# Pairing the later modulation loads and sums, with a re-ordered first stage, in a two-block transformer kernel

## The chip, the cores and the metric

One Trainium2 chip, one core. The metric is the device time of one execution in microseconds, the median of the runs shown. The engines named below: PE multiplies matrices (PEld is its weight load), DVE and ACT work element by element, POOL sets constants, SP issues nearly all DMAs from a queue of its own.

## The reference, cut to what matters

Two transformer blocks of two layers each, on 256 latent and 256 context tokens of width 1024, all in float32. What the change touches is the adaptive norm of the first block: a condition vector gives a shift, a scale and a gate of 1024 values each, for each of two layers, for latent tokens and for context tokens.

```python
def adaln_terms(cond, w_ada, b_ada):
    m = jax.nn.silu(cond) @ w_ada + b_ada        # [1024] @ [1024, 3072]
    return jnp.split(m, 3, axis=-1)
...
for li in range(DEPTH):
    shift_l, scale_l, gate_l = adaln_terms(c, ada_w[li], ada_b[li])
    shift_c, scale_c, gate_c = adaln_terms(c_ctx, ada_w[li], ada_b[li])
    xl = rms_norm(h_lat, norm_w[li]) * (1.0 + scale_l[:, None, :]) + shift_l[:, None, :]
    xc = rms_norm(h_ctx, norm_w[li]) * (1.0 + scale_c) + shift_c
    out_l, out_c = mixer(xl, xc, ...)            # projections, attention, output projection
    h_lat = h_lat + gate_l[:, None, :] * out_l
```

## The kernel before, in words

Every engine runs one program that is written out by hand; semaphores join them. The work is a sequence of weight chunks r = 0, 1, 2, ... of 128x1024 floats (512 KB). For each chunk SP loads it into one of four `raw` buffers (`load_raw`, L757), ACT rounds it into a high part (`split_hi`, L839), DVE subtracts to get the low part (`split_lo`, L1341), and PE forms three products of high and low parts (L2088 to L2090). SP may load chunk r only when the low part of chunk r - 4 is done: `lo_done` must have reached r - 3. The queue of SP is strictly in order, so whatever stands behind a waiting load waits too.

The modulation weights `ada_w` (25 MB) are read as 24 quanta of 256 columns; each is loaded as two halves of 512 KB (`load_ada`, L768) into four buffers `ada_raw`. PE sums a quantum with the condition as a 32-column stationary operand: four products side by side, one in each quarter of the PSUM rows, for each half (`condition`, L2183). A float32 product shows as two records in the trace. ACT copies the sum out (`ada_evacuate`, L881), PE transposes it (`condition_turn`, L2199), DVE adds the four parts and the bias (`ada_finish`, L1482).

The first stage. The first eight quanta give scale and shift of layer 0. x arrives in four tiles of 128 tokens and is transposed column tile by column tile (`turn_x`, L2260: eight groups of four transposes into two PSUM banks `tr`, each copied out by ACT). The norm factors come from DVE, which squares the four tiles as they land. Then four "pairs" follow. Pair p needs quanta 2p and 2p + 1; DVE makes `amod`, then for each of four half tiles (two column tiles, latent and context) a product `ntmp` (L1405), ACT makes the high part `h_hi` (L854), DVE the low part `h_lo` (L1415), and PE multiplies all this with chunk p of the "av" weights (`value_part`: 24 products of 512 columns a pair). In `modulated_norm` the low part of chunk p is made in one piece of 1024 columns; for pairs 1 to 3 it is made between `ada_finish(2p)` and `ada_finish(2p + 1)`.

PE's order in the kernel before, in a pair p with 0 < p < 3: `condition(2p+2)`, six products, `condition_turn(2p+2)`, `condition(2p+3)`, six products, `condition_turn(2p+3)`, twelve products.

After the first stage the sixteen later quanta are summed in eight pairs, at chunk slots 6, 8, ..., 20 (`condition_pair`): PE sums quantum 8 + 2j into columns 0 to 255 of a PSUM bank and quantum 9 + 2j into columns 256 to 511, projects the chunk, and then transposes the bank. SP's order is: four times (two quanta, one chunk), chunks 4 to 7, right behind chunk 7 eleven small and middling loads (constants, vectors for lambda, layer norm, `a_ws`; L788 to L800), chunk 8, modulation pair 0, chunks 9 and 10, modulation pair 1, and so on.

Of the kernel before, what the change touches and what calls it, by code (L numbers as in the profile page):

```python
# [170 lines left out]
NADA = 3 * KT  # L171
ADA_COLS = 256
ADA_FIRST, ADA_ALL, NADA_RAW = 8, 24, 4

# [239 lines left out]
def build_program(nc, t, out):  # L414

    with ExitStack() as ctx:
        def sb(name, shape, dt=F32):
            return ctx.enter_context(nc.sbuf_tensor(name, shape, dt))
# [4 lines left out]
        def sem(name):  # L423
            return ctx.enter_context(nc.semaphore(name))


        with nc.sbuf_tensor("ada_raw", [P, NADA_RAW, KT, ADA_COLS], F32) as ada_raw:
            pass
        m_hi, m_lo = sb("m_hi", [P, KT * TOK], F32R), sb("m_lo", [P, KT * TOK], F32R)
        cond32 = sb("cond32", [P, KT, 32])  # L430
# [107 lines left out]
            sem("misc_in"), sem("stored"))  # L538
        rows_in = sem("rows_in")
        ones_set, eps_set, lam_set = sem("ones_set"), sem("eps_set"), sem("lam_set")  # L540
# [100 lines left out]
        def source_at(r):  # L641

            if r >= RB:
# [11 lines left out]
                       (V_KVN, t["c_kv_norm_w"]))  # L655

        def ada_bank(n):

            return (sc[:, 1, :], ac[:, :])[n % 2]
# [84 lines left out]
        def _(sp):  # L744
# [14 lines left out]
            def load_ada(n):  # L759
# [6 lines left out]
                for half in range(2):  # L766
                    tiles = slice(4 * half, 4 * half + 4)
                    sp.dma_start(ada_raw[:, n % NADA_RAW, tiles, :], src[:, tiles, :])\  # L768
                        .then_inc(ada_in[half][n % NADA_RAW], 16)

            for r in range(HELD):
                load_ada(2 * r)
                load_ada(2 * r + 1)
                load_raw(r)
            for r in range(HELD, RB + LAYERS_2 * C2):
# [8 lines left out]
                if r - 2 in ADA_OF_SLOT:  # L784
                    for n in ada_pair(ADA_OF_SLOT[r - 2]):
                        load_ada(n)
                if r == 7:
# [34 lines left out]
        def _(act):  # L822
# [77 lines left out]

            turned(0, vec[:], tr[:, 0, 0:V_END])
            act.wait_ge(tr_free, 1)
# [3 lines left out]
            def x_turned_to(k):  # L906
                use = TR1_OF[("x", k)]
                turned(use, x_t[:, k, :], tr[:, use % 2, :])

# [4 lines left out]

            for k in range(3):
                x_turned_to(k)
            ada_evacuate(0)
            x_turned_to(3)
            ada_evacuate(1)
            x_turned_to(4)  # L920
            split_hi(0)
            modulated_hi(0, 0)
            x_turned_to(5)
            x_turned_to(6)
            modulated_hi(0, 1)
            x_turned_to(7)
            for pair in range(1, 4):
                ada_evacuate(2 * pair)
                ada_evacuate(2 * pair + 1)
                split_hi(pair)  # L930
                modulated_hi(pair, 0)
                modulated_hi(pair, 1)
            nc.scalar.activation(small[:, 60:61], ones[:, 0:1], ACT.Gelu)
# [392 lines left out]
        def _(dve):  # L1326
# [8 lines left out]
            def split_lo(r):  # L1335
# [6 lines left out]
                last.then_inc(lo_done, 1)  # L1342

            rotations = [0]

# [147 lines left out]
            def modulated_norm(layer, v0, v1, chunk=None):  # L1493
                dve.wait_ge(rs_set, layer + 1)
                for v in range(v0, v1 + 1):
                    u = 2 * KT * layer + v
                    if v < v1:
                        k, half = norm_tile(layer, v)
                        norm_tmp(u, k, (LAT, CTX)[half], amod[:, layer, half, k:k + 1], (LAT, CTX)[half])
                    if chunk is not None and v == v0 + 1:  # L1500
                        split_lo(chunk)
                    if v > v0:
                        k, half = norm_tile(layer, v - 1)
                        norm_lo(u - 1, k, (LAT, CTX)[half], mod[:, layer, k, half:half + 1])

            norm_rsqrt(0, 4)
            for pair in range(4):
                ada_finish(2 * pair)
                if pair:
                    split_lo(pair)  # L1510
                ada_finish(2 * pair + 1)
                dve.wait_ge(ada_set, 2 * pair + 2)
                modulation(0, 2 * pair, 2 * pair + 2, 2 * pair + 2)
                modulated_norm(0, 4 * pair, 4 * pair + 4, chunk=None if pair else 0)
            split_lo(HELD)
# [563 lines left out]
        def _(pe):  # L2079
# [107 lines left out]
            def condition_pair(j):  # L2187

                g = G1_OF[("ada", j)]
                group_bank_free(pe, g, None)  # L2190
                for e, n in enumerate(ada_pair(j)):
                    last = condition_sums(n, bank(g)[:, ADA_COLS * e:ADA_COLS * e + ADA_COLS])
                last.then_inc(proj_done, 1)
# [38 lines left out]
            pe.wait_ge(ident_in, 16)  # L2232
            pe.wait_ge(vec_in, 16 * 9)
            nc.tensor.transpose(tr[:, 0, 0:V_END], vec_rows[0:V_END, :], const[0:V_END, K_ID:K_ID + V_END]).then_inc(tr_done, 1)
            pe.wait_ge(ones_set, 1)
            for n in range(4):
                pe.wait_ge(x_in[n], 16)
            def value_part(name, j, e, tiles=range(4)):
                c = L0_CHUNKS.index((name, j))
                k, (wh, wl) = 2 * j + e, split_views(c)  # L2240
                if e == 0:
                    pe.wait_ge(lo_done, c + 1)
                for n in tiles:
                    tok = slice(P * n, P * n + P)
                    if name == "av":
                        pe.wait_ge(n_lo, 2 * k + n // 2 + 1)
                    if k == 0 and n == 3:
# [14 lines left out]

            turn_x(0)
            turn_x(1)
            turn_x(2)
            pe.wait_ge(cond_set, 1)
            condition(0)
            turn_x(3)
            spread(0, 4)
            condition_turn(0)  # L2270
            condition(1)
            turn_x(4)
            condition_turn(1)
            turn_x(5)
            turn_x(6)
            condition(2)
            turn_x(7)
            for pair in range(4):
                if 0 < pair < 3:
                    condition(2 * pair + 2)  # L2280
                value_part("av", pair, 0, (0, 1))
                if pair < 3:
                    condition_turn(2 * pair + 2)
                    condition(2 * pair + 3)
                value_part("av", pair, 0, (2, 3))
                if pair < 3:
                    condition_turn(2 * pair + 3)
                value_part("av", pair, 1)

# [454 lines left out]
```

## Time and profile before

| what | value |
|---|---|
| median of 3 runs | 1055.52 us (1054.69 to 1056.17) |
| profiled execution | 1054.3 us |
| its span, first to last instruction | 1052.2 us |
| PE busy | 1032.1 us, 98% of the span |
| DVE, ACT busy | 733.7 us, 591.1 us |
| DMA | 165.38 MB, mean 157 GB/s |

The page is made from one execution. The span leaves out what lies around the first and the last instruction, 2.1 us here. PE's busy time counts the modelled ends of pipelined products, so short waits can hide in it; the start of one record to the start of the next is the sharper measure, and the timeline gives it.

### The profile page before, as it was taken

What the parts mean: (1) busy time and instruction counts of PE and PEld (TensorE: products, weight loads), DVE (VectorE), ACT (ScalarE), POOL (GpSimd) and SP (SyncE); (2) the same over time, 40 slices, a digit from 0 to 9 for tenths busy, and PEclk for the clock granted to TensorE, in tenths of its full rate; (3) what the DMA queues carried; (4) which work ended last, traced back from release to release, by engine and by line L of the source; (5) the groups of instructions that cost most, each with busy time, mean ns of one, the idle gap of its engine ahead of it and who ended that gap; (6) DMA issues with size and microseconds to landing.
All of it is one profiled execution on the core that took longest, in us unless ns stands there. A gap on an engine that the chain in (4) does not pass through costs nothing.

```text
span 1052.2 us, 17814 instructions
## 1 busy us (share of the span) xinstructions
PE 1032.1 (98%) x6745; PEld 879.4 (84%) x6745; DVE 733.7 (70%) x1569; ACT 591.1 (56%) x1188; POOL 2.6 (0%) x10
## 2 busy tenths in 40 slices
PE   6999999999999999999999999999999999999997
PEld 3677777788986779989898988889989898888886
DVE  4635576786687657797689775658797688665565
ACT  4534245553365556567667664446578767655444
POOL 0000000000000000000000000000000000000000
PEclk9999999999999999999999999999999999999999
DMA  9998661223333225565555556666455456555662
GB/s 328 274 345 264 183 197 41 81 61 100 100 101 91 61 61 151 137 179 141 141 141 160 160 161 193 188 188 182 132 160 161 128 147 166 155 168 179 184 218 81
DMA packets 203693, 165.38 MB, mean 157 GB/s; under 512 B 7117, under 2 KB 172729, under 8 KB 203609
## 3 DMA queue, kind: packets, MB, share of 16 engines
q1 hardware_dynamic: 203088, 163.28, 53.0%
q8 instruction: 54, 0.88, 0.4%
q0 software_dynamic: 192, 0.66, 0.2%
q10 hardware_dynamic: 328, 0.32, 0.1%
q14 instruction: 31, 0.25, 0.1%
HBM read 163.18 MB, written 1.05 MB: 156 GB/s over the span
## 4 chain that ended last, share of the span: by engine, by line
PE 90%; DVE 6%; ACT 2%; issue 1%; DMA 0%; ACTq 0%; DVEq 0%
PE pj L2088 24%; PE pj L2090 23%; PE pj L2089 23%; DVE w_lo L1341 2%; PE tr L2657 1%; PE pj L2183 1%; PE ac L2450 1%; PE tr L2316 1%; PE ac L2593 1%; PE sc L2436 1%; PE sc L2304 1%; PE ac L2330 1%; ACT w_hi L839 1%; PE sc L2439 1%; PE ac L2596 0%
## 5 line engine op out<-in xcount | busy, mean ns | idle before, releaser
L1341 DVE TENSOR_TENSOR w_lo<-raw,w_hi 128x1024 fp32r<-128x1024 f32 (+2 forms) x258 | 309.4, 1202 | 154.5 <-ACT w_hi L839 153.4
L839 ACT ACTIVATE w_hi<-raw 128x1024 fp32r<-128x1024 f32 (+2 forms) x258 | 267.6, 1040 | 97.4 <-PE pj L2090 90.2
L2088 PE MATMUL pj<-h_hi,w_hi 128*128 128x256 f32 (+1 forms) x960 | 297.1, 309 | 0.5 <-DVE m_lo L1747 0.2
L2090 PE MATMUL pj<-h_hi,w_lo 128*128 128x256 f32 (+1 forms) x960 | 290.5, 303 | 0.0
L2089 PE MATMUL pj<-h_lo,w_hi 128*128 128x256 f32 (+1 forms) x960 | 290.3, 302 | 0.0
L2088 PEld LDWEIGHTS pj<-h_hi,w_hi 128*128 128x128 f32 x960 | 183.2, 191 | 16.5 <-issue 8.4
L2090 PEld LDWEIGHTS pj<-h_hi,w_lo 128*128 128x128 f32 x960 | 183.2, 191 | 7.2
L2089 PEld LDWEIGHTS pj<-h_lo,w_hi 128*128 128x128 f32 x960 | 183.4, 191 | 6.3
L2088 PE MATMUL pj<-w_hi,h_hi 128*128 128x512 f32 x344 | 137.3, 399 | 0.4 <-DVE h_lo L1415 0.4
L2090 PE MATMUL pj<-w_hi,h_lo 128*128 128x512 f32 x344 | 134.2, 390 | 0.0
L2089 PE MATMUL pj<-w_lo,h_hi 128*128 128x512 f32 x344 | 134.2, 390 | 0.0
L2088 PEld LDWEIGHTS pj<-w_hi,h_hi 128*128 128x128 f32 x344 | 64.6, 188 | 17.4 <-issue 4.9
L2090 PEld LDWEIGHTS pj<-w_hi,h_lo 128*128 128x128 f32 x344 | 64.6, 188 | 13.9
L2089 PEld LDWEIGHTS pj<-w_lo,h_hi 128*128 128x128 f32 x344 | 64.7, 188 | 12.2
L2088 PE MATMUL pj<-m_hi,w_hi 128*128 128x256 f32 (+1 forms) x160 | 51.5, 322 | 1.1 <-DVE work L1761 0.8
L2090 PE MATMUL pj<-m_hi,w_lo 128*128 128x256 f32 (+1 forms) x160 | 50.4, 315 | 0.0
L2089 PE MATMUL pj<-m_lo,w_hi 128*128 128x256 f32 (+1 forms) x160 | 50.3, 315 | 0.0
L860 ACT ACTIVATE prob_t<-tr 128x512 f32<-128x512 f32 (+2 forms) x56 | 26.2, 518 | 42.6 <-PE tr L2316 40.3
L2088 PE MATMUL pj<-w_hi,m_hi 128*128 128x512 f32 x104 | 40.7, 392 | 0.0
L2090 PE MATMUL pj<-w_hi,m_lo 128*128 128x512 f32 x104 | 40.5, 390 | 0.0
L2089 PE MATMUL pj<-w_lo,m_hi 128*128 128x512 f32 x104 | 40.5, 389 | 0.0
L2088 PEld LDWEIGHTS pj<-m_hi,w_hi 128*128 128x128 f32 x160 | 30.4, 190 | 5.0 <-DVE work L1761 1.7
(376 smaller groups left out, 1479.6 us busy)
## 6 DMA issues: line engine op xcount, KB each, us to landing
raw<-in_w_in_dram SPq DMA_DIRECT2D x152, 512.0 KB, 3.8
ada_raw<-in_ada_w_dram SPq DMA_DIRECT2D x48, 512.0 KB, 8.4
raw<-in_even_w_in_dram SPq DMA_DIRECT2D x28, 512.0 KB, 7.0
raw<-in_w_branch_dram SPq DMA_DIRECT2D x24, 512.0 KB, 3.6
raw<-in_w_out_dram SPq DMA_DIRECT2D x16, 512.0 KB, 4.3
raw<-in_odd_w_in_dram SPq DMA_DIRECT2D x11, 512.0 KB, 4.0
raw<-in_even_w_out_dram SPq DMA_DIRECT2D x8, 512.0 KB, 3.8
raw<-in_odd_w_out_dram SPq DMA_DIRECT2D x8, 512.0 KB, 3.9
```

The lines of the kernel that those rows point to most:

```text
L839: last = nc.scalar.activation(hi, src, ACT.Copy)
L860: nc.scalar.activation(dst, src, ACT.Copy).then_inc(tr_free, 1)
L1341: last = nc.vector.tensor_tensor(lo, src, hi.bitcast(F32), ALU.subtract)
L2088: nc.tensor.matmul(dst, lh, rh, start=first, stop=False)
L2089: nc.tensor.matmul(dst, lh, rl, start=False, stop=False)
L2090: return nc.tensor.matmul(dst, ll, rh, start=False, stop=final)
L2183: last = nc.tensor.matmul(sums[32 * c:32 * c + 32, :], cond32[:, 4 * half + c, :], ada_raw[:, n % NADA_RAW, 4 * half + c, :], start=half = ...
L2304: nc.tensor.matmul(sc[:, a, unit_cols(u)], q_e[rows, h, P * i:P * i + P], k_e[rows, h, keys], start=True, stop=True).then_inc(sc_done, 1)
L2316: last = nc.tensor.transpose(tr[:, use % 2, P * j:P * j + P], src[:, P * j:P * j + P], ident)
L2330: last = nc.tensor.matmul(ac[:, P * i:P * i + P], prob_t[:, u % 2, P * j:P * j + P], v_e[:, n, P * h:P * h + P], start=(j == 0), stop=(j = ...
L2436: nc.tensor.matmul(sc[:, e, :], qn_o[:, 2 * hp + e, q], kn_o[:, 2 * hp + e, :], start=True, stop=False)
L2439: last = nc.tensor.matmul(sc[:, e, :], qr_o[rows, hp, q], kr_o[rows, :], start=False, stop=True)
```

## The change

It has three parts.

1. The first stage starts in another order. PE transposes the first five column tiles of x token tile by token tile, as each lands, into five banks (`x_bank`: the two `tr` banks and the three `pj` banks), and the small vectors go to bank `ac`; the other three column tiles follow after the first condition sums. PE's, ACT's and DVE's orders in the four pairs change: in pair p PE does six products, turn(2p+2), six products, condition(2p+3), six products, turn(2p+3), six products, condition(2p+4).
2. The low part of chunks 0 to 3 is made in two halves of 512 columns (`split_lo_half`), after the second and after the fourth `ntmp` of its pair. PE's products wait on the first half for the first column tile (`lo_half`) and on the second half (`lo_done`) for the other.
3. The sixteen later quanta are loaded in pairs: two transfers of 1 MB (rows of 512 columns) in place of four of 512 KB, into `ada_wide`, which takes the place of `ada_raw`; PE sums 512 columns with one product in place of two of 256 columns.

```diff
+X_EARLY = 5
...
+        def x_bank(k):
+            return pj[:, k - 2, :] if 2 <= k < X_EARLY else tr[:, TR1_OF[("x", k)] % 2, :]
...
+            def load_ada_pair(j):
+                n = ada_pair(j)[1]
+                sp.wait_ge(*sums_ready(n - NADA_RAW))
+                q = ADA_QUANTUM[n - 1]
+                c0 = ADA_COLS * (q % 12)
+                src = t["ada_w"][q // 12].rearrange("(k p) m -> p k m", p=P)[:, :, c0:c0 + 2 * ADA_COLS]
+                for half in range(2):
+                    tiles = slice(4 * half, 4 * half + 4)
+                    sp.dma_start(ada_wide[:, j % 2, tiles, :], src[:, tiles, :]).then_inc(ada_in[half][2 * (j % 2)], 16)
...
                 if r - 2 in ADA_OF_SLOT:
-                    for n in ada_pair(ADA_OF_SLOT[r - 2]):
-                        load_ada(n)
+                    load_ada_pair(ADA_OF_SLOT[r - 2])
... (ACT, after the first four column tiles of x)
             ada_evacuate(0)
-            x_turned_to(3)
+            x_turned_to(4)
+            x_turned_to(5)
             ada_evacuate(1)
-            x_turned_to(4)
             split_hi(0)
+            x_turned_to(6)
             modulated_hi(0, 0)
-            x_turned_to(5)
-            x_turned_to(6)
+            ada_evacuate(2)
             modulated_hi(0, 1)
             x_turned_to(7)
             for pair in range(1, 4):
-                ada_evacuate(2 * pair)
                 ada_evacuate(2 * pair + 1)
                 split_hi(pair)
                 modulated_hi(pair, 0)
+                if pair < 3:
+                    ada_evacuate(2 * pair + 2)
                 modulated_hi(pair, 1)
... (DVE)
+            def split_lo_half(r, e):
+                dve.wait_ge(hi_done, r + 1)
+                part = slice(e * WEL // 2, (e + 1) * WEL // 2)
+                (src, hi, lo), = split_pieces(r)
+                nc.vector.tensor_tensor(lo[:, part], src[:, part], hi[:, part].bitcast(F32), ALU.subtract)\
+                    .then_inc((lo_half, lo_done)[e], 1)
...
-                    if chunk is not None and v == v0 + 1:
-                        split_lo(chunk)
+                    if chunk is not None and v in (v0 + 1, v0 + 3):
+                        split_lo_half(chunk, (v - v0) // 2)
...
                 ada_finish(2 * pair)
-                if pair:
-                    split_lo(pair)
                 ada_finish(2 * pair + 1)
...
-                modulated_norm(0, 4 * pair, 4 * pair + 4, chunk=None if pair else 0)
+                modulated_norm(0, 4 * pair, 4 * pair + 4, chunk=pair)
... (PE)
-                for e, n in enumerate(ada_pair(j)):
-                    last = condition_sums(n, bank(g)[:, ADA_COLS * e:ADA_COLS * e + ADA_COLS])
+                for half in range(2):
+                    pe.wait_ge(ada_in[half][2 * (j % 2)], 16 * (ADA_FIRST // NADA_RAW + j // 2 + 1))
+                    for c in range(4):
+                        last = nc.tensor.matmul(bank(g)[32 * c:32 * c + 32, :], cond32[:, 4 * half + c, :],
+                                                ada_wide[:, j % 2, 4 * half + c, :], start=half == 0, stop=half == 1)
...
+            for i in (0, 2, 1, 3):
+                if i == 3:
+                    pe.wait_ge(vec_in, 16 * 9)
+                    nc.tensor.transpose(ac[:, 0:V_END], vec_rows[0:V_END, :], const[0:V_END, K_ID:K_ID + V_END])\
+                        .then_inc(tr_done, 1)
+                pe.wait_ge(x_in[i], 16)
+                for k in range(X_EARLY):
+                    last = nc.tensor.transpose(x_bank(k)[:, P * i:P * i + P], x_tok[:, i, P * k:P * k + P], ident)
+                    if i == 3:
+                        last.then_inc(tr_done, 1)
...
             for pair in range(4):
-                if 0 < pair < 3:
-                    condition(2 * pair + 2)
                 value_part("av", pair, 0, (0, 1))
                 if pair < 3:
                     condition_turn(2 * pair + 2)
-                    condition(2 * pair + 3)
                 value_part("av", pair, 0, (2, 3))
                 if pair < 3:
+                    condition(2 * pair + 3)
+                value_part("av", pair, 1, (0, 1))
+                if pair < 3:
                     condition_turn(2 * pair + 3)
-                value_part("av", pair, 1)
+                value_part("av", pair, 1, (2, 3))
+                if pair < 2:
+                    condition(2 * pair + 4)
```

## Rows read from the trace of the kernel before

**Rows 1.** The page: busy us, share of the span, instructions.
```profile
PE 1032.1 (98%) x6745; PEld 879.4 (84%) x6745; DVE 733.7 (70%) x1569; ACT 591.1 (56%) x1188; POOL 2.6 (0%) x10
```

**Rows 2.** Waits of PE over the whole span: us in total, times, longest.
```profile
PE tr L2234 <- DMA scr<-in_c_kv_norm_w_dram: 8.9, 1, 8.9
...
PE sc L2183 <- DMA ada_raw<-in_ada_w_dram: 0.5, 1, 0.5
...
PE pj L2088 <- DVE h_lo L1415: 0.4, 1, 0.4
```

**Rows 3.** Timeline of PE in the first stage: start us, us.
```profile
28.53 0.39 PE L2089 MATMUL tr<-w_lo,h_hi 128*128 128x512 f32 x1
28.76 0.39 PE L2090 MATMUL tr<-w_hi,h_lo 128*128 128x512 f32 x1
29.07 1.07 PE L2183 MATMUL sc<-ada_raw,cond 128*32 128x256 f32 x16
...
37.45 1.07 PE L2183 MATMUL sc<-ada_raw,cond 128*32 128x256 f32 x16
...
46.34 0.47 PE L2088 MATMUL pj<-w_hi,h_hi 128*128 128x512 f32 x1 [0.44 <-DVE h_lo L1415]
```

**Rows 4.** SP's issues: start us, us the issue took.
```profile
17.37 1.32 SPq L768 DMA_DIRECT2D ada_raw<-in_ada_w_dram  x1
...
44.03 0.37 SPq L757 DMA_DIRECT2D raw<-in_even_w_in_dram  x1
...
50.28 0.61 SPq L800 DMA_DIRECT2D prob<-in_a_ws_dram  x1
51.67 0.38 SPq L757 DMA_DIRECT2D raw<-in_even_w_in_dram  x1
...
55.12 0.86 SPq L768 DMA_DIRECT2D ada_raw<-in_ada_w_dram  x1
```

**Rows 5.** DMA landing of the issues at 17.37, then 55.12: us after the issue.
```profile
ada_raw<-in_ada_w_dram SPq DMA_DIRECT2D x1, 512.0 KB, 10.9
...
ada_raw<-in_ada_w_dram SPq DMA_DIRECT2D x1, 512.0 KB, 8.8
```

**Rows 6.** Timeline of DVE around the last pair of the first stage.
```profile
42.78 1.23 DVE L1341 TENSOR_TENSOR w_lo<-raw,w_hi 128x1024 fp32r<-128x1024 f32 x1 [2.02 <-ACT w_hi L839]
43.92 0.17 DVE L1482 TENSOR_REDUCE mod<-ac 128x4 f32<-128x16 f32 x1
...
44.59 0.87 DVE L1405 SCALAR_TENSOR_TENSOR ntmp<-x_t,amod,sc 128x256 f32<-128x256 f32 x2
45.71 0.49 DVE L1415 SCALAR_TENSOR_TENSOR h_lo<-ntmp,mod,h_hi 128x256 fp32r<-128x256 f32 x1 [0.25 <-ACT h_hi L854]
```

**Rows 7.** DVE groups by form: busy us, mean ns of one.
```profile
L1582 DVE TENSOR_TENSOR m_lo<-work,m_hi 128x512 fp32r<-128x512 f32 x8 | 5.2, 685 | 0.7 <-ACT m_hi L999 0.7
```

**Rows 8.** Windows: length, granted clock, DMA share, GB/s.
```profile
50.00:51.00 1.00, 1.00 0.35 131
53.00:54.00 1.00, 1.00 0.89 255
58.00:62.00 4.00, 1.00 1.10 348
63.00:65.00 2.00, 1.00 1.06 385
```

**Rows 9.** Timeline of PE at the first later modulation pair.
```profile
62.91 1.93 PE L2183 MATMUL pj<-ada_raw,cond 128*32 128x256 f32 x32
64.77 0.50 PE L2088 MATMUL pj<-h_hi,w_hi 128*128 128x512 f32 x1
```

**Rows 10.** PEld at the first modulation sum, sets of four side by side.
```profile
12.60 0.20 PEld L2183 LDWEIGHTS sc<-ada_raw,cond 128*32 128x32 f32 x4 [0.23 <-issue]
13.03 0.20 PEld L2183 LDWEIGHTS sc<-ada_raw,cond 128*32 128x32 f32 x4 [0.23 <-issue]
```

**Rows 11.** The line of the x transposes: ns min/median/max, first and last start.
```profile
L2260 PE MATMUL tr<-const,work x32: 272/300/474, 9.3 to 20.6; 128*128 128x128 f32 x32
```

More of the change, by code:

```diff
@@ L428, in build_program @@
             pass
+        with nc.sbuf_tensor("ada_wide", [P, NADA_RAW // 2, KT, 2 * ADA_COLS], F32) as ada_wide:
+            pass
         m_hi, m_lo = sb("m_hi", [P, KT * TOK], F32R), sb("m_lo", [P, KT * TOK], F32R)
@@ L538, in build_program @@
             sem("misc_in"), sem("stored"))
-        rows_in = sem("rows_in")
+        rows_in, lo_half = sem("rows_in"), sem("lo_half")
         ones_set, eps_set, lam_set = sem("ones_set"), sem("eps_set"), sem("lam_set")
@@ L899, in _ @@
                 nc.scalar.dma_start(vec_rows[c0:c0 + src.shape[0], :], src).then_inc(vec_in, 16)
-            turned(0, vec[:], tr[:, 0, 0:V_END])
+            turned(0, vec[:], ac[:, 0:V_END])
             act.wait_ge(tr_free, 1)
@@ L907, in x_turned_to @@
                 use = TR1_OF[("x", k)]
-                turned(use, x_t[:, k, :], tr[:, use % 2, :])
+                turned(use, x_t[:, k, :], x_bank(k))
             def value_evacuate(name, n):
@@ L913, in value_evacuate @@
                 nc.scalar.activation(dst, value_bank(name, n), ACT.Gelu if name == "av" else ACT.Copy).then_inc(value_free, 1)
-            for k in range(3):
+            for k in range(4):
                 x_turned_to(k)
             ada_evacuate(0)
-            x_turned_to(3)
+            x_turned_to(4)
+            x_turned_to(5)
             ada_evacuate(1)
-            x_turned_to(4)
             split_hi(0)
+            x_turned_to(6)
             modulated_hi(0, 0)
-            x_turned_to(5)
-            x_turned_to(6)
+            ada_evacuate(2)
             modulated_hi(0, 1)
@@ L2232, in _ @@
             pe.wait_ge(ident_in, 16)
-            pe.wait_ge(vec_in, 16 * 9)
-            nc.tensor.transpose(tr[:, 0, 0:V_END], vec_rows[0:V_END, :], const[0:V_END, K_ID:K_ID + V_END]).then_inc(tr_done, 1)
+            for i in (0, 2, 1, 3):
[8 more added lines that the diff above has]
+                        last.then_inc(tr_done, 1)
             pe.wait_ge(ones_set, 1)
-            for n in range(4):
-                pe.wait_ge(x_in[n], 16)
             def value_part(name, j, e, tiles=range(4)):
@@ L2240, in value_part @@
                 k, (wh, wl) = 2 * j + e, split_views(c)
-                if e == 0:
+                if e == 0 and name == "av":
+                    pe.wait_ge(lo_half, j + 1)
+                else:
                     pe.wait_ge(lo_done, c + 1)
@@ L2246, in value_part @@
                         pe.wait_ge(n_lo, 2 * k + n // 2 + 1)
+                    if name == "av" and k == 0 and n == 0:
+                        pe.wait_ge(tr_free, TR1_OF[("x", X_EARLY - 1)] + 1)
                     if k == 0 and n == 3:
@@ L2261, in turn_x @@
                 last.then_inc(tr_done, 1)
-            turn_x(0)
-            turn_x(1)
-            turn_x(2)
             pe.wait_ge(cond_set, 1)
             condition(0)
-            turn_x(3)
             spread(0, 4)
             condition_turn(0)
+            turn_x(5)
             condition(1)
-            turn_x(4)
+            turn_x(6)
             condition_turn(1)
-            turn_x(5)
-            turn_x(6)
+            turn_x(7)
             condition(2)
-            turn_x(7)
             for pair in range(4):
-                if 0 < pair < 3:
-                    condition(2 * pair + 2)
                 value_part("av", pair, 0, (0, 1))
```

## The prediction

> **What bounds the kernel now.** I read the page first: PE is busy for 1032.1 of 1052.2 us [rows 1]. So an edit pays only where PE waits, or where PE itself gets less to do. Next the waits of PE: 8.9 us until the first vectors land, then nothing above 0.8 us; among the rest 0.5 us on a modulation quantum and 0.4 us on `h_lo` [rows 2]. All the time that scheduling can win lies before 52 us.
>
> Then the timeline of PE in the first stage. One product of 512 columns takes 0.23 us from start to start; the condition sum of pair 1 starts at 29.07 and that of pair 2 at 37.45, so a pair takes 8.38 us [rows 3]. A pair's work is 24 products (5.5), two sums of 1.1 each and two turns of 0.25, with 0.1 for each of two switches: 8.4 us. PE is the bound inside the stage. Only the last pair waits: its first product starts at 46.34 after 0.44 us [rows 3].
>
> Last, SP. Chunk 7 is issued at 44.03, the eleven loads behind it end at 50.28 + 0.61 = 50.89, chunk 8 goes at 51.67, and the last transfer of modulation pair 0 at 55.12 [rows 4]. Why 44.03: the low part of chunk 3 is done at 42.78 + 1.23 = 44.01 [rows 6], and SP waits for just that. The last transfer of pair 0 lands 8.8 us after its issue [rows 5], at 63.92. PE starts that pair at 62.91, needs the last quarter about 1.4 us later at 64.3, and is through at 64.77 [rows 9]. **PE runs into the first later pair with 0.4 us to spare.** The reader is to see this: a low part that PE does not wait for sets when SP may go on.
>
> **Part 1, the first stage.** The transposes before the first sum get cheaper, but condition(4) needs its second half, which is issued at 17.37 and lands 10.9 us later [rows 4, 5], at 28.27. Before, PE comes to it at 29.07 [rows 3]. After, I lay the steps out with the durations above: PE gets there at about 27.5, sums the first half, waits 0.3 us and is through at 28.8, 1.3 us ahead of before. This lead is then spent. In the new order a pair's second turn stands six products before its end, not twelve. From turn(2p+1) the path is: turn and hand-over 0.44, DVE from the reduction to `ntmp` 44.59 - 43.92 = 0.67 [rows 6], two `ntmp` 0.79, half a low part 0.61 (a 128x512 subtraction is 0.685 from start to end [rows 7], 0.61 to the next one, as 1.23 stands to 1.14 in [rows 6]), `h_lo` 0.49 [rows 6], hand-over 0.06: 3.05 us. PE has six products left, and a sum in pairs 0 and 1: 1.45 + 1.1 after the turn's 0.24. So:
> - pair 1 starts at 28.8; six products, turn, six products, sum, six products = 1.45 x 3 + 0.24 + 1.1 = 5.7, so turn(5) is at 34.5;
> - pair 2 starts at 34.5 + 3.05 = 37.5 (PE waits 0.3), turn(7) is at 43.2;
> - pair 3 starts at 43.2 + 3.05 = 46.25 (PE waits 1.35).
>
> Before it started at 46.34 [rows 3]. The first stage ends where it did: **0.0 us**, with 0.5 either way for the hand-overs.
>
> **Part 2, the half low parts.** In the last pair DVE now does, from `ntmp` at 43.2 + 0.44 + 0.67 = 44.3: two `ntmp`, a half, `h_lo`, `ntmp`, `h_lo`, `ntmp`, then the second half. That is 0.79 + 0.61 + 4 x 0.395 = 2.98, so it starts at 47.3 and is done at 48.0. Before, the whole low part was done at 44.01 [rows 6]. `lo_done` reaches 4 **4.0 us later**, and chunk 7 is issued at 48.0 instead of 44.03. Behind it in SP's queue stand the eleven loads, chunk 8 and modulation pair 0. The eleven take 6.86 us of issuing, so chunk 8 goes at 54.9 (its own wait, the low part of chunk 4, was over at 51.67 before [rows 4] and moves little). PE does not wait for chunk 7 itself: its first use is two chunks further on, so for it the delay costs nothing.
>
> For pair 0 it costs this. The issue is 3.2 us later (4.0 less the 0.78 us that SP idled before chunk 8). The landing could move by that or by the full 4.0: the queues are nearly full in both cases, at 0.89 of an engine's share at 53 us [rows 8], so most of the gap closed in SP's queue does not shorten the line. I take 3.6. Rows of 512 columns move faster: 385 GB/s at 63 to 65 us, when chunks 9 and 10 with their 2 KB rows are on the way, against 348 at 58 to 62, when the 1 KB rows of pair 0 are [rows 8]. For the 2.1 MB of a pair that is 6.0 against 5.6, so -0.4 (bounds 0 and -0.45). The last half lands at 63.92 + 3.2 = 67.1. PE then has 0.95 us of sums left, because half of the pair's work hangs on the last transfer, no longer a quarter: it is through at 68.1, where the row has 64.77 [rows 9]. **+3.3 us** (bounds: 67.7, so +2.9, and 68.9, so +4.1). What follows at that slot is late alike: ACT copies the sum out later, and chunk 10's high part behind it; DMA and PE then run with the distances of before, and no wait of 0.5 us or more follows in which PE could give the time back [rows 2].
>
> The Trainium skill (DMA: Bandwidth & Descriptors, section "Bandwidth", under "Measured") asks for transfers of 1 MiB or more for 75% of peak, and gives 2.0 us plus bytes at 436 GB/s for one. Here 512 KB transfers already stream at 348 GB/s, since the queue holds several at once [rows 8]. By the page's formula four small ones, one after another, would cost 12.8 us and two large ones 8.8, and pair 0 would come 4 us earlier; by the rows it is 0.4.
>
> **Part 3, sums of 512 columns.** 32 records take 64.77 - 62.91 = 1.86 us [rows 9], four side by side 0.232. Is that columns or instructions? At the first sum PE still runs at half its clock: sets of four start 0.43 apart, 12.60 and 13.03 [rows 10], twice 0.215. So at least 0.215 of 0.232 is columns passing, which a wider product does not save. Merged, sets of four take 0.43 to 0.46, four of them 1.72 to 1.86: a gain of 0 to 0.14 a pair. I take 0.08, times eight: **-0.6 us** (0 to -1.1). Would instructions bind, a pair's 1.86 would halve and the kernel win 7 us; the doubling at half clock speaks against it.
>
> **The sum.** 0.0 + 3.3 - 0.6 = +2.7. On the profiled execution's own 1054.3 that is 1057.0. The median of the runs shown lies 1.2 above it, so 1055.5 + 2.7 = 1058.2.
>
> **The rivals.**
> - *The late loads are made good before pair 0* (the other side). Place: the stretch of the eleven small loads, where the DMA share is only 0.35 at 50 us [rows 8]. If pair 0 owes its landing to other work in the queues and not to SP's issue, the delay vanishes. It decides at a landing of 63.9 or earlier, half a sum before PE would otherwise be through. Then only part 3 is left: 1055.5 - 0.6 = 1054.9. For it: slack in the queues between 44 and 53. Against it: they are full from 55 on, at 1.10 [rows 8], and 4 us of work cannot be found behind. 15%. The page's formula above would give this case.
> - *The first stage does end earlier.* The hand-overs between pairs are hidden, the lead of 1.3 us stays, and chunk 7 goes 1.3 earlier too: 1058.2 - 1.3 = 1056.9. For it: PE is ahead at 28.8. Against it: 3.05 against 2.8 and 1.7 us of cover. 10%.
> - *PE falls to half its clock.* The transposes of x take 474 ns at first and 272 later [rows 11]: PE starts slow after its 8.9 us of idling, and the sums at 12.60 and 13.03 are still slow [rows 10]. After the change PE has holes of about 1 us around 17 to 19.5, and about 3 us of waiting at 63 to 67. If the clock falls there and stays low for as long as at the start, 8.9 to about 13.5, half of 4.6 us is lost: 1058.2 + 2.3 = 1060.5. The Trainium skill (TensorE: Matmul & The Clock Gate, section "What's actually happening") says that the clock starts at half, rises with sustained activity and falls after idling; the slow start agrees. Against it: PE works in pieces through these holes. 10%.
>
> **How the numbers follow.** Forecast 60% (its own range 1057.0 to 1059.4), the three rivals 15, 10 and 10, anything else 5. The predicted time is 1058.2. The range takes in the first two rivals and reaches toward the third: 1054.8 to 1060.0, which leaves out some 15%. A measurement of this kernel can tell about 0.2%, 2.1 us, from no change. Slower by more: four fifths of the forecast (0.47), the clock (0.10) and a little of the second rival: 0.58. Within: the rest of the forecast 0.13, most of the first rival 0.12, of the second 0.08: 0.33. Faster by more: 0.09, for what I have not seen.
>
> **What would show it.** The profile after should have: the first product of pair 3 at 46.3 behind a wait of 1.3 us on `h_lo`; chunk 7 issued at 48.0; a wait of PE on `ada_wide` near 63 to 67 in two pieces, the pair through at 68; and then sums of 1.7 to 1.8 us a pair with no such wait. If chunk 7 goes at 44 or the pair's last half lands by 64, my main step is wrong. If the sums take 0.95 us, part 3 is.

## The result, and the profile after

The changed kernel takes 1063.35 us (median of 4 runs, 1063.07 to 1064.09), the kernel before 1055.7 beside it (1054.69 to 1056.17): ratio 1.0075, interval 1.0057 to 1.0092. It is 7.65 us slower, where 2.7 were forecast, and 3.3 above the top of the range. The profiled execution took 1064.09 us, its span is 1062.3 us.

The page of the kernel after: busy time, the granted clock in 40 slices, and the group of the wide sums.
```profile
PE 1038.7 (98%) x6617; PEld 879.5 (83%) x6617; DVE 733.0 (69%) x1573; ACT 590.8 (56%) x1188; POOL 2.6 (0%) x10
...
PEclk9989999999999999999999999999999999999999
...
ada_wide<-in_ada_w_dram SPq DMA_DIRECT2D x16, 1024.0 KB, 8.9
```
PE has 128 instructions fewer than in [rows 1] and is busy 6.6 us longer. Work that became slower, not only waiting, is in the difference; the clock's 8 in the third slice (53 to 80 us) says where.

The waits of PE over the whole span: us in total, times, longest.
```profile
PE tr L2266 <- DMA work<-in_x_dram: 5.4, 1, 5.4
PE pj L2217 <- DMA ada_wide<-in_ada_w_dram: 3.1, 2, 1.5
PE pj L2111 <- DVE h_lo L1440: 2.0, 3, 1.4
...
PE pj L2111 <- DVE w_lo L1366: 1.0, 1, 1.0
```
Against [rows 2], two waits are new, `ada_wide` with 3.1 and the half low part with 1.0, and that on `h_lo` grew from 0.4 to 2.0.

The timeline of PE after: start us, us, and in brackets the idle time before and what ended it.
```profile
13.35 0.64 PE L2206 MATMUL sc<-ada_raw,cond 128*32 128x256 f32 x8 [0.63 <-DMA ada_raw<-in_ada_w_dram]
14.29 2.07 PE L2253 MATMUL sc<-const,col 128*128 128x128 f32 x8 [0.30 <-DVE col L1387]
...
29.68 1.07 PE L2206 MATMUL sc<-ada_raw,cond 128*32 128x256 f32 x16
...
31.08 0.47 PE L2111 MATMUL pj<-w_hi,h_hi 128*128 128x512 f32 x1 [0.33 <-DVE h_lo L1440]
...
48.61 0.47 PE L2111 MATMUL pj<-w_hi,h_hi 128*128 128x512 f32 x1 [1.35 <-DVE h_lo L1440]
...
64.86 0.39 PE L2113 MATMUL pj<-h_hi,w_lo 128*128 128x512 f32 x1
66.78 1.06 PE L2217 MATMUL pj<-ada_wide,cond 128*32 128x512 f32 x8 [1.53 <-DMA ada_wide<-in_ada_w_dram]
69.39 1.93 PE L2217 MATMUL pj<-ada_wide,cond 128*32 128x512 f32 x8 [1.54 <-DMA ada_wide<-in_ada_w_dram]
71.26 0.80 PE L2111 MATMUL pj<-h_hi,w_hi 128*128 128x512 f32 x1
...
72.70 0.63 PE L2111 MATMUL pj<-h_hi,w_hi 128*128 128x512 f32 x1
...
73.98 0.63 PE L2111 MATMUL pj<-h_hi,w_hi 128*128 128x512 f32 x1
75.26 0.61 PE L2111 MATMUL pj<-h_hi,w_hi 128*128 128x512 f32 x1
```
Three things are to be seen. The wait ahead of pair 3 is 1.35 us long, as forecast to the digit, but its end is at 48.61 and not at 46.25, since pair 1's condition sum already starts at 29.68. PE waits for modulation pair 0 in two pieces of 1.5 us. And the sum behind the second piece takes 1.87 us from start to start where the one behind the first takes 1.06; every third product then starts 1.28 us on, 0.43 each, where [rows 3] have 0.23. PE is at half its clock.

The windows of PE after: length, then the busy time and count of PE, PEld, DVE, ACT and POOL, the granted clock, DMA share, GB/s.
```profile
10.00:15.00 5.00, 3.33 (x27) 1.98 (x26) 3.71 (x18) 3.29 (x8) 0.00 (x0) 0.93 1.10 353
15.00:20.00 5.00, 5.00 (x40) 3.74 (x40) 0.64 (x4) 1.84 (x4) 0.00 (x0) 0.73 1.09 357
65.00:70.00 5.00, 1.92 (x14) 0.38 (x16) 0.82 (x3) 0.60 (x1) 0.00 (x0) 0.89 1.06 388
70.00:75.00 5.00, 5.00 (x17) 2.98 (x10) 1.23 (x1) 1.54 (x2) 0.00 (x0) 0.50 1.05 385
75.00:80.00 5.00, 5.00 (x24) 4.09 (x23) 0.36 (x2) 0.88 (x2) 0.00 (x0) 0.93 1.09 354
...
438.00:440.00 2.00, 2.00 (x11) 2.00 (x11) 1.79 (x8) 0.00 (x0) 0.00 (x0) 0.50 0.00 0
```
The lower of the two clock levels (1.2 GHz of 2.4) is granted at about 14.3 to 17.7 us, from 69 to 76, and once more around 439. In the kernel before PE is slow only at its start [rows 10]; the windows around pair 0 show 1.00 [rows 8].

DVE and SP after, at the last pair of the first stage.
```profile
46.59 0.87 DVE L1430 SCALAR_TENSOR_TENSOR ntmp<-x_t,amod,sc 128x256 f32<-128x256 f32 x2
47.38 0.69 DVE L1366 TENSOR_TENSOR w_lo<-raw,w_hi 128x512 fp32r<-128x512 f32 x1
...
49.56 0.69 DVE L1366 TENSOR_TENSOR w_lo<-raw,w_hi 128x512 fp32r<-128x512 f32 x1
```
```profile
50.27 0.37 SPq L763 DMA_DIRECT2D raw<-in_even_w_in_dram  x1
...
56.51 0.61 SPq L816 DMA_DIRECT2D prob<-in_a_ws_dram  x1
57.16 0.59 SPq L763 DMA_DIRECT2D raw<-in_even_w_in_dram  x1
57.79 2.52 SPq L786 DMA_DIRECT2D ada_wide<-in_ada_w_dram  x2
```
The second half low part starts 2.97 us behind the first `ntmp` (2.98 forecast) and ends at 50.25; SP issues chunk 7 at 50.27. In [rows 4] that is 44.03: 6.24 us later, of which 2.3 are the stage's own delay and 4.0 the place of the low part in DVE's order.

**Where 10.1 us of span went.** (1) Pair 3 starts 48.61 - 46.34 = 2.3 us late. (2) At full clock the last sum of pair 0 would take 0.93, so PE would be through at 69.39 + 0.93 = 70.32; less 64.77 [rows 9] and less 2.3 that is 3.3 us of waiting. (3) The sum took 0.94 more, and the ten steps from the start at 71.26 to that at 75.69 take 4.43 us where they took 2.40 before: 3.0 us at half clock. (4) The stretch near 439 costs 1.5. Product by product, the start after less the start before (the lag, from here on) is 2.3 at 60 us, 8.6 at 76, 8.7 at 425 and 10.1 from 445 to the end. Sum 10.1 = 1062.3 - 1052.2. The medians lie only 7.65 apart: the profiled execution of before was 1.4 below its median and that of after 0.7 above, and 0.3 lies outside the spans.

Two of the four terms are not the same in every execution. Four profiled kernels have the first stage of the kernel before (before, late7_busy, late_chunk7, wide_only, explained below), and their pair 3 starts at 46.34, 46.58, 46.73 and 47.37; four have that of the changed kernel as it stands (small_first, after_busy, stage_only, after), and theirs starts at 47.87, 48.07, 48.08 and 48.61. So 2.3 compares the earliest with the latest; the means are 1.4 apart. The stretch near 439 comes and goes as well (see early_x_sq), and it is not shown that the change brings it.

### The profile page after: what moved, and what is told of

Same layout as the page of the kernel before. It is cut to its first block, busy times and chain, and to the rows that moved or that the text cites. A ratio compares the mean times of both kernels' runs of the same rounds, so it can differ in the third digit from the quotient of the medians.

```text
span 1062.3 us, 17552 instructions
## 1 busy us (share of the span) xinstructions
PE 1038.7 (98%) x6617; PEld 879.5 (83%) x6617; DVE 733.0 (69%) x1573; ACT 590.8 (56%) x1188; POOL 2.6 (0%) x10
## 4 chain that ended last, share of the span: by engine, by line
PE 88%; DVE 6%; DMA 2%; issue 2%; ACT 1%; SPq 0%; DVEq 0%; ACTq 0%
PE pj L2111 23%; PE pj L2113 22%; PE pj L2112 22%; DVE w_lo L1358 2%; PE tr L2690 1%; PE pj L2217 1%; PE ac L2483 1%; PE tr L2349 1%; PE ac L2626 1%; PE sc L2469 1%; PE sc L2337 1%; PE ac L2363 1%; DMA ada_wide<-in_ada_w_dram 1%; ACT w_hi L855 1%; DMA work<-in_ctx_dram 1%
## 5 line engine op out<-in xcount | busy, mean ns | idle before, releaser
L1358 DVE TENSOR_TENSOR w_lo<-raw,w_hi 128x1024 fp32r<-128x1024 f32 (+2 forms) x254 | 304.7, 1202 | 152.3 <-ACT w_hi L855 151.2
```

Source lines behind the costliest of these rows:

```text
L1358: last = nc.vector.tensor_tensor(lo, src, hi.bitcast(F32), ALU.subtract)
```

## The experiments

Twelve kernels, each measured beside the kernel before, whose median was 1055.0 beside the first eight and 1055.1 beside the last four (after_busy, after_turn7, mixed, early_x_sq). Ratios are against it. Lags are from the profiled execution alone, against the profile before.

**stage_only and wide_only: which part?** The first is the changed kernel without part 3, the second the kernel before with part 3 alone (its edit is shown).
```diff
-                    for n in ada_pair(ADA_OF_SLOT[r - 2]):
-                        load_ada(n)
+                    load_ada_pair(ADA_OF_SLOT[r - 2])
...
-                for e, n in enumerate(ada_pair(j)):
-                    last = condition_sums(n, bank(g)[:, ADA_COLS * e:ADA_COLS * e + ADA_COLS])
+                for half in range(2):
...
+                                                ada_wide[:, j % 2, 4 * half + c, :], start=half == 0, stop=half == 1)
```


> Parts 1 and 2 without part 3 (the new first stage, later quanta as 512 KB transfers and 256-column sums). If the loss comes from the first stage and from what it does to SP's queue: chunk 7 issued at 50 us, PE waits 3 to 4 us at the first later sum, its clock falls there, +7 to +9 us against before. If it comes from part 3: within 2 us of before.

> Part 3 alone on the kernel before (pairs of 512 columns, 1 MB transfers, first stage as before). My theory: chunk 7 is issued at 44.0 as before, pair 0 is through by 65.0, each later pair takes 1.7 to 1.8 us instead of 1.86: -0.3 to -0.8 us against before. Rival (the merged sums or the 1 MB transfers themselves cost time, since half a pair hangs on the last transfer): a wait of PE on ada_wide in slot 6 and +1 us or more.

Measured: stage_only 1062.69 (1061.37 to 1064.51), ratio 1.0069 (1.0054 to 1.0084); wide_only 1054.31 (1053.41 to 1056.64, 10 runs), ratio 0.9995 (0.9985 to 1.0004). The loss is in parts 1 and 2. The median of wide_only is 0.7 us lower, as was expected, but the interval takes in no change, and the sums did not get shorter. Part 3 on the timeline of PE in wide_only, first later pair:
```profile
63.89 1.92 PE L2206 MATMUL pj<-ada_wide,cond 128*32 128x512 f32 x16
65.74 0.50 PE L2100 MATMUL pj<-h_hi,w_hi 128*128 128x512 f32 x1
```
Sixteen wide records take 1.85 us; the 32 narrow ones took 1.86 [rows 9]. Half as many instructions over the same columns gain nothing: the lag of wide_only is 1.0 us at pair 3, through its first stage, which is as before, and between 1.0 and 1.1 from there to the end, over all eight pairs.

**small_first: is it SP's queue behind chunk 7?** The changed kernel, with the eleven small loads issued ahead of chunk 7 and not behind it, so that they go while SP would wait for `lo_done`.
```diff
             for r in range(HELD, RB + LAYERS_2 * C2):
-                load_raw(r)
                 if r == 7:
                     sp.dma_start(const[:, 0:K_PRC] ...
...
+                load_raw(r)
```


> The changed kernel with the eleven small loads issued ahead of chunk 7 instead of behind it. If the late chunk 7 costs its time through the loads queued behind it: pair 0 is issued near 54.5 instead of 57.8, PE's waits on ada_wide and the half clock after them vanish, and 5 to 6 us of the 7.7 come back (+1.5 to +2.5 us against before, what the first stage itself lost). Rival (the clock is lost in the first stage and stays disturbed, or the DMA engines are the bound anyway): less than 2 us comes back.

Measured: 1056.16 (1054.36 to 1057.33, 10 runs), ratio 1.0006 (0.9996 to 1.0015). SP and PE in this kernel:
```profile
49.52 4.83 SPq L763 DMA_DIRECT2D raw<-in_even_w_in_dram  x2
54.40 1.30 SPq L786 DMA_DIRECT2D ada_wide<-in_ada_w_dram  x2
```
```profile
28.90 1.07 PE L2206 MATMUL sc<-ada_raw,cond 128*32 128x256 f32 x16
...
47.87 0.47 PE L2111 MATMUL pj<-w_hi,h_hi 128*128 128x512 f32 x1 [1.35 <-DVE h_lo L1440]
...
64.43 1.92 PE L2217 MATMUL pj<-ada_wide,cond 128*32 128x512 f32 x16
```
Chunk 7 still goes at 49.5, but pair 0 goes at 54.40 and not at 57.79; PE does not wait for it, and the clock is 1.00 from 65 to 75. Some 7 of the 7.65 us hang on the order in one queue. The stage is late all the same: pair 3 at 47.87, 1.5 behind the profile before. What is left above before goes with the clock: the three executions with a mean granted clock of 0.998 or 0.999 took 1054.36 to 1054.62, the seven with 0.995 to 0.997 took 1055.82 to 1057.33.

**late_chunk7: does the late chunk do it alone?** The kernel before; SP waits for DVE's fifteenth `h_lo` ahead of chunk 7.
```diff
             for r in range(HELD, RB + LAYERS_2 * C2):
+                if r == 7:
+                    sp.wait_ge(n_lo, 15)
                 load_raw(r)
```


> The kernel before, with one wait more: SP holds chunk 7 until the second last low part of the first stage is made, 47.8 us instead of 44.0. Nothing of PE, ACT or DVE is changed. My theory: the last transfer of pair 0 lands 3.2 to 3.8 us later, PE waits about 3 us in slot 6 and the kernel is 2.9 us slower, and 2 to 3.4 us more if PE's clock falls in that wait. Rival (queue slack absorbs it): within 0.5 us of before.

Measured: 1060.40 (1059.65 to 1061.91), ratio 1.0044 (1.0027 to 1.0061), 5.4 us above before. SP, PE and the window behind the wait:
```profile
48.19 0.37 SPq L757 DMA_DIRECT2D raw<-in_even_w_in_dram  x1
```
```profile
68.96 1.08 PE L2185 MATMUL pj<-ada_raw,cond 128*32 128x256 f32 x8 [0.87 <-DMA ada_raw<-in_ada_w_dram]
```
```profile
70.00:75.00 5.00, 5.00 (x16) 3.94 (x13) 1.23 (x1) 1.54 (x2) 0.00 (x0) 0.50 1.10 352
```
One transfer issued 4.2 us later, in a kernel that is otherwise the one before, brings the wait and then the half clock. In this profile, that of the slowest of the four executions, the lag is 0.4 at 60 us and 7.7 at 76: at full clock the last quarter of the sum would be through at 68.96 + 0.47 = 69.43, so 4.3 are waiting, in four pieces of 0.78 to 1.19, and 3.0 are the half clock. The median cannot be split like that.

**after_busy and late7_busy: is the clock a cost of its own?** The changed kernel and late_chunk7, each with 14 spare products into an unused bank ahead of pair 0; their results go nowhere. They fill 3.3 us in which PE would wait.
```diff
+                if s == ADA_SLOTS[0]:
+                    for _ in range(14):
+                        nc.tensor.matmul(sc[:, 1, :], h_hi[:, 0, 0:P], h_hi[:, 0, :], start=True, stop=True)
                 if s in ADA_OF_SLOT:
                     condition_pair(ADA_OF_SLOT[s])
```


> The changed kernel with 14 spare products of 512 columns (3.2 us, result unused) ahead of the first later sum, inside PE's wait for its data. If the half clock after that wait costs PE 3 us: clock 1.00 from 60 to 80 us, and the shift against before at 72 us falls from 8.6 to between 5.5 and 6.5. Rival (the wait would only get longer, as the profile of late7_busy with its later last landing leaves open): 8 or more.

> late_chunk7 with 14 spare products of 512 columns (3.2 us, result unused) ahead of the first later sum, inside the stretch in which PE waits for its data anyway. If half of the loss of late_chunk7 is the clock that falls after the wait: the clock stays at 1.00 from 60 to 80 us and 2.5 to 3.4 us of its 5.4 come back. Rival (the slow stretch at 69 to 75 us has another cause or costs nothing): same as late_chunk7 or slower.

Measured: after_busy 1061.18 (1059.81 to 1061.77), ratio 1.0053 (1.0039 to 1.0066), 2.2 us below the changed kernel; late7_busy 1060.41 (1058.55 to 1061.40), ratio 1.0051 (1.0036 to 1.0066), no better than late_chunk7. PE of after_busy, and its window behind the wait:
```profile
64.54 3.33 PE L2397 MATMUL sc<-h_hi 128*128 128x512 f32 x14
68.15 1.06 PE L2217 MATMUL pj<-ada_wide,cond 128*32 128x512 f32 x8 [0.28 <-DMA ada_wide<-in_ada_w_dram]
70.78 1.06 PE L2217 MATMUL pj<-ada_wide,cond 128*32 128x512 f32 x8 [1.56 <-DMA ada_wide<-in_ada_w_dram]
```
```profile
70.00:75.00 5.00, 4.22 (x22) 2.85 (x23) 1.23 (x1) 1.55 (x2) 0.00 (x0) 1.00 1.05 387
```
With work in the first gap the clock stays at 1.00 from 60 to 80 us in both kernels, so the gaps are what lowered it. The time won is less than 3.0, because the last transfer landed later: the last sum starts 21.05 us behind chunk 7's issue and not 19.12, and in late7_busy 21.88 and not 20.77. Why it lands later is open. The lag of after_busy at 76 us is 7.0, between the 5.5 to 6.5 expected and the 8 of the rival. Of the 3.2 us between its profile and that of after, 0.5 lie in the first stage, 1.0 at pair 0, and 1.5 are the stretch near 439, which after_busy does not have; so of the 2.2 between the medians perhaps half is won at pair 0. For late7_busy the profiles say more than the medians: its lag at 76 us is 5.7 against 7.7 in late_chunk7, and then it loses 1.5 in a stretch at half clock at 433 to 437 us that late_chunk7 does not have. The two kernels show that the gaps cause the fall; its price of 3.0 is read from the durations above, not from these times.

**after_turn7: is it the place of the last turn?** The changed kernel; in pair 2 alone, condition(7) and its turn stand six products earlier, as before.
```diff
+                if pair == 2:
+                    condition(2 * pair + 3)
                 value_part("av", pair, 0, (2, 3))
-                if pair < 3:
+                if pair < 2:
                     condition(2 * pair + 3)
+                if pair == 2:
+                    condition_turn(2 * pair + 3)
                 value_part("av", pair, 1, (0, 1))
-                if pair < 3:
+                if pair < 2:
                     condition_turn(2 * pair + 3)
```


> The changed kernel with the sum and turn of quantum 7 taken six products earlier in pair 2, as the kernel before has them. By my hand-over sum the wait of 1.35 us before pair 3 vanishes and lo_done reaches 4 about 1.4 us earlier: 1.4 us faster than the changed kernel, up to 3 if the wait in slot 6 gets short enough to keep the clock. Rival (the hand-over is hidden behind something else): no change.

Measured: 1059.16 (1056.95 to 1061.74, 8 runs), ratio 1.0035 (1.0024 to 1.0046), 4.2 below the changed kernel. The wait ahead of pair 3 is gone and chunk 7 goes at 47.28, 3.0 earlier. PE still waits 1.62 and 1.56 us for pair 0, and the clock still falls behind it. More than the expected 1.4 came back, and the profile shows why: up to pair 2 the program is that of after, but the clock does not fall at 14 us, and the sum of pair 1 starts at 28.06.
```profile
13.72 1.16 PE L2253 MATMUL sc<-const,col 128*128 128x128 f32 x8 [0.28 <-DVE col L1387]
```
The eight executions of this one kernel also give the clock a price in time: four with a mean granted clock of 0.997 or 0.998 took 1056.95 to 1058.56, four with 0.993 to 0.995 took 1059.75 to 1061.74, 2.9 us more in the mean, for whatever stretches at half clock they had more.

**whole_lo: is it the second half low part?** The changed kernel; both halves stand back to back behind the second `ntmp`.
```diff
-                    if chunk is not None and v in (v0 + 1, v0 + 3):
-                        split_lo_half(chunk, (v - v0) // 2)
+                    if chunk is not None and v == v0 + 1:
+                        split_lo_half(chunk, 0)
+                        split_lo_half(chunk, 1)
```


> The changed kernel with both half low parts of a chunk made back to back after the second ntmp of the pair. lo_done reaches 4 about 1.6 us earlier, the first product of pair 3 comes 0.6 later. If the landing of pair 0 sets the time: about 1.6 us faster than the changed kernel (1061.7). Rival (the pair's hand-over in the first stage sets it): 0.6 us slower than the changed kernel.

Measured: 1060.27 (1059.24 to 1062.21), ratio 1.0053 (1.0038 to 1.0068). Chunk 7 goes at 49.63, but each pair now waits for `h_lo` longer, pair 3 until 50.14 behind 1.95 us, and another stretch at half clock follows (50.5 to 53.9 us). PE reaches pair 0 at 68.28 and does not wait; the lag is 5.4 there and stays so to the end. The median is 3.1 below the changed kernel, where 1.6 were expected; the profile has no stretch near 439, which can be half of that. The delay is mostly taken elsewhere: this version trades one wait for another.

**early_x and warm: why does the first stage start late?** early_x is the kernel before with only the tile-wise transposes of part 1. warm is small_first with 15 spare transposes where PE would wait near 10 to 20 us; their results go nowhere.
```diff
+            def busy(dst, n):
+                for _ in range(n):
+                    nc.tensor.transpose(dst, x_tok[:, 0, 0:P], ident)
+
+            busy(sc[:, 0, 0:P], 5)
...
             condition(0)
+            busy(sc[:, 0, 0:P], 4)
             spread(0, 4)
...
             turn_x(7)
+            busy(pj[:, 0, 0:P], 6)
             condition(2)
```


> The kernel before with only the tile-by-tile transposes of the first five column tiles of x; the pairs' order, the low parts and the later quanta as before. My first reckoning (DMA landings bind by 20 us): 0.0, within 0.3 us of before. If the holes that this order leaves in PE cost the clock: half clock near 14 to 18 us and +0.5 to +2 us.

> small_first with 15 spare transposes of a tile of x (results unused, overwritten later) put into PE's holes of the first 20 us: five before the first sum, four before the norm's spread, six before the third sum. If the slow stretch at 14 to 17 us comes from PE's holes and costs the stage its time: the granted clock stays at 1.00 from about 11 us on, the first product of pair 3 starts 0.8 to 1.6 us earlier than in small_first (47.9), and the kernel is within 0.3 us of before or faster. Rival (the holes' clock loss is hidden behind DMA landings): no change against small_first, or slower by the spare work.

Measured: early_x 1055.68 (1053.88 to 1056.91, 10 runs), ratio 1.0005 (0.9996 to 1.0014); warm 1054.51 (1054.18 to 1055.84, 10 runs), ratio 0.9998 (0.9989 to 1.0008). PE of early_x, then of warm:
```profile
11.54 1.08 PE L2187 MATMUL sc<-ada_raw,cond 128*32 128x256 f32 x8 [0.41 <-DVE cond L1465]
...
13.83 2.08 PE L2231 MATMUL sc<-const,col 128*128 128x128 f32 x8
...
30.19 1.07 PE L2187 MATMUL sc<-ada_raw,cond 128*32 128x256 f32 x16
```
```profile
13.59 1.06 PE L2253 MATMUL sc<-const,col 128*128 128x128 f32 x8
...
27.87 1.22 PE L2206 MATMUL sc<-ada_raw,cond 128*32 128x256 f32 x16
...
46.81 0.47 PE L2111 MATMUL pj<-w_hi,h_hi 128*128 128x512 f32 x1 [1.35 <-DVE h_lo L1440]
```
Eight transposes with the same operands take 2.08 us in early_x and 1.06 in warm. Doing the transposes as each tile lands leaves PE in pieces. In early_x it stays slow from its first work to 17.0 us (half a sum takes 1.08 where it takes 0.64 in the changed kernel), while the kernel before is at full clock from 13.5 on; in the changed kernel, small_first and after_busy the clock is up at about 11 us and down again from 14 to 17. It is not so in every execution: with the same program up to there stage_only and after_turn7 do the eight transposes in 1.16 us. With the holes filled, pair 1's sum starts at 27.87, against 28.90 in small_first, and the first sum at 11.21 against 11.30: 1.0 us of the start is the clock. after_turn7, which had full clock without any spare work, has that sum at 28.06.

**mixed: the parts together.** warm with the reordering of after_turn7.

> warm (small loads first, spare transposes in the early holes) with quantum 7 taken six products earlier in pair 2. Pair 3 starts 1.3 us earlier than in warm: 1.0 to 1.4 us faster than warm, 1053.3, the fastest of all. Rival (DMA landings or SP's queue take over as the bound of the stage or of slot 6): within 0.5 us of warm.

Measured: 1054.71 (1053.28 to 1057.03, 12 runs), ratio 0.9994 (0.9986 to 1.0003). The loss is gone, but the 1.0 to 1.4 us expected below warm did not come: pair 0's second half is waited for again (1.15 us), and the stage's lead goes into that, from a lag of -0.8 at pair 3 to +0.6 behind pair 0. By the clock of the executions, the eight at 0.998 or 0.999 took 1053.28 to 1055.05, the four at 0.996 or 0.997 took 1055.63 to 1057.03.

**early_x_sq: the stretch near 430.** In early_x a slow stretch stands near 430 us, as near 439 in the changed kernel. Windows of early_x, columns as above:
```profile
430.00:432.00 2.00, 2.00 (x12) 2.00 (x11) 1.69 (x11) 0.00 (x0) 0.00 (x0) 0.50 0.00 0
```
Just ahead of it in the changed kernel PE does 16 products of one column for the sum of squares of a norm. The kernel adds eight spare transposes in each later norm; they are computed for nothing.
```diff
+                if s >= 2:
+                    for _ in range(8):
+                        nc.tensor.transpose(sc[:, 0, 0:P], ones[:], ident)
                 pe.wait_ge(sq_done, KT * s)
```


> early_x with eight spare transposes between the single-column sums of squares of the later norms (near 428 us, and again in the next layer). If the half clock near 430 to 434 us, which costs 1.5 us in about half of early_x's executions, comes from the stretch of 16 one-column products: no execution shows it any more, mean clock 0.998 in all, median 0.3 to 1 us below early_x after the 0.9 us that the spare work costs at most. Rival (it has another cause): it still shows in about half of the executions.

Measured: 1056.78 (1055.29 to 1058.17, 11 runs), ratio 1.0012 (1.0003 to 1.0021), by the ratios 0.7 us above early_x. The profiled execution has clock 1.00 there, but early_x itself has executions without the stretch, and two of the eleven here still have a mean clock of 0.996, which can be this stretch or another. The spare work also costs more than the 0.9 us allowed for: the lag grows by 0.8 at this norm and by 0.8 again at the next layer's, 1.6 in all, as much as the stretch costs where it comes. So the medians could show no gain, and the cause of the stretch stays open. Seven of the fourteen profiles have it (after, stage_only, small_first, after_turn7, mixed, early_x, late7_busy), seven do not (before, wide_only, late_chunk7, after_busy, whole_lo, warm, early_x_sq); late7_busy has the first stage of the kernel before, so no part of the change is needed for it.

## Why the prediction was wrong, point by point

| step | forecast | measured (profiled execution) |
|---|---|---|
| wait ahead of pair 3 | 1.35 us | 1.35 |
| first `ntmp` to second half low part | 2.98 | 2.97 |
| chunk 7 to the last landing of pair 0 | 19.1 | 59.13 + 10.2 - 50.27 = 19.1 |
| pair 0 waited for, beyond the stage | +3.3 | +3.3 |
| **first stage** | **0.0 (0.5 either way)** | **+2.3 (means of four and four profiles: +1.4); +0.5 in warm** |
| **half clock behind the wait** | a rival, +2.3, 10% | **+3.0** |
| sums of 512 columns | -0.6 | 0.0 |
| later stretch at half clock | not seen | +1.5 |

**The step that failed first is "the first stage ends where it did: 0.0 us".** It had pair 1's sum start at 27.5, with 0.3 of waiting in it, and the first product of the pair at 28.8; the sum started at 29.68 and the product at 31.08, 2.3 late. One microsecond of that is the clock, as warm shows. Another 0.8 lies ahead of the stage: the first sum starts at 12.08 in this execution and at 11.30 in small_first, with the same program up to there. The rest, 0.4, is mostly a wait of 0.33 on `h_lo` that the forecast does not have at this pair. From there to pair 3 it is 48.61 - 31.08 = 17.53 us, and the forecast has 17.45: inside the pairs it was right. The prediction named the holes of PE around 17 to 19.5 and did not price them in the sum, although [rows 10, 11] show what the same work costs at half clock.

**The second is the sum itself, which holds the wait but not what follows it.** The mechanism at pair 0, the late low part, SP's queue and the two pieces of waiting, was right in place; late_chunk7 and small_first show it from both sides. Its size, 3.3, was hit with luck. The forecast let the line from chunk 7's issue to the last landing shrink from 19.9 by 0.4 for SP's closed idling and 0.4 for the wide rows. Without the idling but with narrow loads it measured 70.70 - 49.75 = 20.95 in stage_only, 1.1 longer and not 0.4 shorter, and with wide ones 19.1, 1.9 shorter and not 0.4: two misses of 1.5 that cancel. But a wait of 3 us that PE had not had before is followed by 6.8 us at half clock, and that nearly doubles its price. The third rival had the place and the size about right (2.3 against 3.0) and a chance of 10%. Its argument against, that PE works in pieces through the holes, was the wrong way round: 1.1 us of work between two gaps did not hold the clock. The Trainium skill (TensorE: Matmul & The Clock Gate, section "What's actually happening") lets the clock fall after idling; the fall to 0.50 at 70 to 75 us agrees, and it came though neither gap is over 1.54 us.

**Part 3** was taken at 0.08 us a pair from a range of 0 to 0.14; the lower end is what wide_only shows. Instructions do not bind there, as the doubling at half clock had said. Its wider rows do move faster, 388 GB/s at 65 to 70 us against 353 in the same window before, but PE had not waited for them. The forecast also slipped in pricing them: 2.1 MB at its own 385 GB/s are 5.45 us and not 5.6. The Trainium skill (DMA: Bandwidth & Descriptors, section "Anatomy of one DMA — SWDGE (gpsimd) path") gives its formula of 2.0 us plus bytes at 436 GB/s for single transfers of the gpsimd path; the 4 us that the prediction worked out from it for a line of transfers did not come, only the 1.9 between stage_only and after.

The first rival, late loads made good, is refuted by the landing at 69.3; the second, an earlier end of the stage, by pair 3 at 48.61.

## What to carry to other kernels

When a producer's step is moved past others, follow every transfer that is released by it and all that stands behind that transfer in its queue; here eleven small loads behind one waiting load cost more than the change could win, and putting them ahead of it gave nearly all of it back. Price a new wait of PE of a few microseconds with the clock that it loses behind it, and look at short pieces of work between gaps as gaps. Fewer, wider products over the same columns are no gain, and starting work as early as its data lands can lower the clock under the work that matters. And when a stretch at half clock comes in some executions only, compare the granted clock of each execution before you split a difference of medians.

## What the runs showed of the hardware that was not expected

Two gaps of 1.53 and 1.54 us with 1.1 us of sums between them were enough for a fall to 1.2 GHz that lasted 6.8 us; in late_chunk7 it fell inside the last of four, of 1.19, 0.78, 0.87 and 0.87 us, with 0.6 us of sums between them. Fourteen products of 512 columns in the first gap prevented it in both kernels. A stretch of 3.4 us at half clock can also come late in the kernel, at 428 to 441 us, with PE busy 2.00 of 2.00 us; it is in seven of the fourteen profiles, and nothing tried here explains it. And 1 MB transfers landed 1.9 us sooner than twice as many of 512 KB in the same place in the queue, without a gain in the kernel's median (1063.35 against 1062.69).
